# Five norms' sums of squares on four column groups of TensorE, with a copy and a fold

## The reference

```python
def rmsnorm(x, g):
    x32 = x.astype(jnp.float32)
    y = x32 * lax.rsqrt(jnp.mean(x32 * x32, axis=-1, keepdims=True) + EPS)
    return (y * g.astype(jnp.float32)).astype(x.dtype)

x = x + mix(rmsnorm(x, norm_mix_g[l])) @ w_out
x = x + conv_ffn(rmsnorm(x, norm_ffn_g[l]), ffn_w_up[l], ffn_conv_w[l], ffn_conv_b[l], ffn_w_down[l])
```

## Time and profile before

| | |
|---|---|
| median of three runs | 1513.62 us (1512.83 to 1514.57) |
| profiled execution, its own time | 1513.27 us |
| its span, first to last instruction | 1511.5 us |
| TensorE busy | 1461.0 us |
| VectorE busy | 1082.4 us |
| ScalarE busy | 732.3 us |
| mean granted TensorE clock | 0.989 of full |
| bytes moved | 274.79 MB, 182 GB/s |

### The profile page before, as it was taken

How to read it: one execution, slowest core, us unless ns; L and a number is a source line. 1 busy time by engine, 2 the same in 40 slices (tenths; PEclk the granted TensorE clock), 3 DMA queues, 4 the chain that set the end, 5 groups by cost and what they waited for, 6 DMA issues and landing times.

```text
span 1511.5 us, 26784 instructions
## 1 busy us (share of the span) xinstructions
PE 1461.0 (97%) x10486; PEld 1298.9 (86%) x10486; DVE 1082.4 (72%) x1659; ACT 732.3 (48%) x949; POOL 6.8 (0%) x19
## 2 busy tenths in 40 slices
PE   7989999999999999999999999899999999999997
PEld 7887889999987889999888779679999899799997
DVE  6774778778756787777766666667777768677775
ACT  6553545444545555445555433545444433454442
POOL 0000000000000000000000000000000000000000
PEclk9999999999999999999999999999999999999999
DMA  7433645555556344554526566055455554555551
GB/s 279 154 140 130 259 167 189 197 177 189 190 200 259 132 176 169 194 192 168 215 85 223 199 248 237 20 199 199 172 190 182 203 201 167 185 200 174 192 180 43
DMA packets 39677, 274.79 MB, mean 182 GB/s; under 512 B 4528, under 2 KB 5680, under 8 KB 6960
## 3 DMA queue, kind: packets, MB, share of 16 engines
q1 hardware_dynamic: 38304, 265.82, 48.9%
q0 software_dynamic: 720, 6.82, 1.2%
q10 hardware_dynamic: 576, 1.05, 0.2%
HBM read 272.62 MB, written 1.05 MB: 181 GB/s over the span
## 4 chain that ended last, share of the span: by engine, by line
PE 86%; DVE 7%; DMA 3%; ACT 3%; issue 2%; SPq 0%; DVEq 0%; ACTq 0%
PE L L1750 25%; PE D L1750 16%; PE L L1938 15%; PE L L1944 8%; PE N L1938 5%; DMA raw<-in_units 3%; PE N L1944 3%; PE M L1838 2%; DVE wlo L972 2%; PE N L1846 2%; PE D L1938 1%; PE D L2212 1%; PE N L2225 1%; DVE arena L1049 1%; PE D L1944 1%
## 5 line engine op out<-in xcount | busy, mean ns | idle before, releaser
L1750 PE MATMUL L<-h_all,whi 128*128 128x256 f32 (+1 forms) x1392 | 286.5, 305 | 14.9 <-DVE wlo L1258 7.0
L972 DVE TENSOR_TENSOR wlo<-raw,whi 128x2048 fp32r<-128x2048 f32 x106 | 242.3, 2286 | 76.9 <-ACT whi L492 76.5
L492 ACT ACTIVATE whi<-raw 128x2048 fp32r<-128x2048 f32 x106 | 202.0, 1909 | 120.7 <-PE L L1750 75.6
L1938 PE MATMUL L<-h_all,whi 128*128 128x512 f32 x992 | 252.7, 396 | 4.4 <-DVE h_all L1021 3.2
L1750 PEld LDWEIGHTS L<-h_all,whi 128*128 128x128 f32 x1392 | 228.3, 197 | 32.4 <-issue 16.4
L1134 DVE TENSOR_TENSOR wlo<-raw,whi 128x2048 fp32r<-128x2048 f32 x96 | 219.6, 2288 | 39.3 <-ACT whi L626 39.3
L1938 PEld LDWEIGHTS L<-h_all,whi 128*128 128x128 f32 x992 | 178.7, 190 | 41.4 <-DVE h_all L1021 5.1
L1750 PE MATMUL L<-h_all,wlo 128*128 128x256 f32 (+1 forms) x696 | 209.7, 301 | 0.0
L626 ACT ACTIVATE whi<-raw 128x2048 fp32r<-128x2048 f32 x96 | 182.9, 1905 | 0.0
L1750 PE MATMUL D<-hd_hi,whi 128*128 128x256 f32 x640 | 181.3, 283 | 0.0
L1750 PE MATMUL D<-hd_hi,wlo 128*128 128x256 f32 x640 | 181.1, 283 | 0.0
(11 more groups left out here) (305 smaller groups left out, 2269.0 us busy)
## 6 DMA issues: line engine op xcount, KB each, us to landing
raw<-in_units SPq DMA_DIRECT2D x250, 1024.0 KB, 4.9
arena<-in_band POOLq DMA_DIRECT2D x1, 2304.0 KB, 10.3
arena<-in_nax POOLq DMA_DIRECT2D x1, 1536.0 KB, 6.7
t<-in_mem ACTq DMA_DIRECT2D x4, 256.0 KB, 5.8
raw<-in_units SPq DMA_DIRECT2D x4, 256.0 KB, 5.4
x<-in_x SPq DMA_DIRECT2D x1, 1024.0 KB, 9.1
t<-in_ctx POOLq DMA_DIRECT2D x1, 1024.0 KB, 5.3
arena<-in_ctx POOLq DMA_DIRECT2D x1, 1024.0 KB, 7.4
```

Of the source, the lines that this page charges most:

```text
L492: A.activation(whi[weight_slot(v)][:], raw[v % RING][:], ACT.Copy).then_inc(unit_hi, 1)
L972: V.tensor_tensor(wlo[w][:], raw[v % RING][:], whi[w][:].bitcast(FP), ALU.subtract) \
L1750: ins = mm(dst, w[a], h[b], start=start and n == 0, stop=stop and n == 2, skip_group_check=True)
L1938: mm(bank[:], w[0][:, k, part * P:part * P + P], h_all[:, k, 0:512], start=k == 0, stop=False, skip_group_check=True)
```

## The change

TensorE's eight full products of a norm become eight products with 32 columns of ones, on four column groups: group g sums blocks 2g and 2g+1 into the output rows 32g to 32g+31 (`partial_sums`). VectorE copies the result to `var` (`gather`), and TensorE adds the four groups by one full product of ones with the copy (`fold_sums`). As each partial sum stands in 32 rows, the fold gives 32 times the sum, and the variance divides by 32 D. It applies to norms 1 to 5 above; the norms before ffn2, o_b and ffn3, the final one and the one after ffn1 keep `sums`. The places change too: for norms 3 and 5 all products now stand in the first chunk of the feed-forward layer and none between the jobs of a_out and b_out; the fold stands behind that chunk's `rest`. For norm 2 the fold stands behind the first job of a_out, its variance step behind the evacuation of that job, and ScalarE's root behind it too. For norm 4 the fold stands between kv_k0 and b_qm; for norm 1 right behind the partial sums.

```diff
@@ scalar
             jobs("mv1")
-            root(rs2)
             def a_rows(n, j):
+                if n == 0:
+                    root(rs2)
                 square(x, n)
@@ vector
+            def gather():
+                gathered[0] += 1
+                dve.wait_ge(R["ss_part"], gathered[0])
+                V.tensor_copy(var[:], N0[:, 0:T]).then_inc(R["ss_copy"], 1)
...
-            def residual(name, gate=None, g=None):
+            def residual(name, gate=None, g=None, behind_first=None):
...
+                if behind_first:
+                    hooks[0] = behind_first
@@ vector, ffn
                 upto(u0 + 2)
                 if not scaled:
-                    stat()
+                    gather()
+                    stat(32 * D)
                     dve.wait_ge(R["rs_done"], stats[0])
@@ vector, norms 2 and 3
-            stat()
+            gather()
             modulation(0, 0, 16, 1, [(0, 8, 1, "mix_w2", 0), (1, 8, 0, "mix_w2", 0)], fin=1)
-            residual("a_out", g=lambda k: vc("ffn_g", k))
+            residual("a_out", g=lambda k: vc("ffn_g", k), behind_first=lambda: stat(32 * D))
@@ tensor
-            def last_sums():
-                sums(2)
-                sums(3)
+            def partial_sums():
+                for i in range(2):
+                    for g in range(4):
+                        if i == 0:
+                            pe.wait_ge(R["sq_done"], 4 * stats[0] + g + 1)
+                        ins = mm(N0[32 * g:32 * g + 32, 0:T], ones[:, 0:32], sq[:, 2 * g + i, :],
+                                 start=i == 0, stop=i == 1)
+                ins.then_inc(R["ss_part"], 1)
+                parts[0] += 1
+            def fold_sums():
+                pe.wait_ge(R["ss_copy"], parts[0])
+                mm(N0[:, 0:T], ones[:, 0:P], var[:], start=True, stop=True).then_inc(R["ss_done"], 1)
+                stats[0] += 1
...
                     for part in range(2):
                         rest(w, ffn_bank(0, part), part)
+                    if mid:
+                        fold_sums()
...
             job(JOBS["mk0"][0], True, ready=first_ready)
-            stat()
+            partial_sums()
+            fold_sums()
             jobs("mv0")
...
-            stat()
-            residual("a_out", lambda k: MIX["memA"] + (k // 3 + 1 if k < 6 else 0), [6, 7, 0, 1, 2, 3, 4, 5], late=True)
-            ffn("ffn0", 0, last_sums, behind=None)
-            jobs("kv_k0", fresh=True, mid=stat)
+            partial_sums()
+            residual("a_out", lambda k: MIX["memA"] + (k // 3 + 1 if k < 6 else 0), [6, 7, 0, 1, 2, 3, 4, 5],
+                     after={0: fold_sums})
+            ffn("ffn0", 0, partial_sums, behind=None)
+            jobs("kv_k0", fresh=True, mid=partial_sums)
+            fold_sums()
             jobs("b_qm", fresh=True)
...
-            residual("b_out", b_mixed, [6, 7, 0, 1, 2, 3, 4, 5], late=True, begun=B_BEGUN)
-            ffn("ffn1", 1, last_sums, behind=boundary_sums)
+            residual("b_out", b_mixed, [6, 7, 0, 1, 2, 3, 4, 5], begun=B_BEGUN, after={})
+            ffn("ffn1", 1, partial_sums, behind=boundary_sums)
```

More of the change, by code:

```diff
@@ L384, in build @@
         R = {n: sem(n) for n in (
-            "ones_set", "sc_clear", "cc_ready", "rows_clear", "ada_out", "ada_turned", "ctx_hi", "ctx_lo", "piece_hi", "piece_lo", "sq_done", "ss_done", "rv_done", "rs_done", "t_done",
+            "ones_set", "sc_clear", "cc_ready", "rows_clear", "ada_out", "ada_turned", "ctx_hi", "ctx_lo", "piece_hi", "piece_lo", "sq_done", "ss_part", "ss_copy", "ss_done", "rv_done", "rs_done", "t_done",
             "h_hi_done", "h_lo_done", "rs_turn", "ctx_t", "sg_done", "v1_done", "rs1_done", "x_ready", "mod_ready", "q_silu", "o_sig",
@@ L958, in _ @@
             V = nc.vector
-            steps, made, stats, applied, rounded = [0], [0], [0], [0], [0]
+            steps, made, stats, applied, rounded, gathered = [0], [0], [0], [0], [0], [0]
             def step(ins):
@@ L1120, in evac @@
                     return V.scalar_tensor_tensor(d[1], b[:, T:512], gate(2 * n + 1), d[1], ALU.mult, ALU.add)
-                jobs(name, evac, {} if g is None else {n: (lambda n=n: rows(n - 1)) for n in range(1, 4)})
+                hooks = {} if g is None else {n: (lambda n=n: rows(n - 1)) for n in range(1, 4)}
+                if behind_first:
+                    hooks[0] = behind_first
+                jobs(name, evac, hooks)
                 if g is not None:
@@ L1744, in _ @@
             mm = nc.tensor.matmul
-            stats, h_in = [0], [0]
+            stats, parts, h_in = [0], [0], [0]
             def mm3(dst, w, h, start, stop):
@@ L1849, in sums, with residual @@
                     stats[0] += 1
-            def stat():
-                for i in range(4):
-                    sums(i)
-            def last_sums():
-                sums(2)
-                sums(3)
-            def residual(name, mixed, order=range(KB), late=False, begun={}):
+            def partial_sums():
[11 more added lines that the diff above has]
+                stats[0] += 1
+            def residual(name, mixed, order=range(KB), begun={}, after=None):
                 if name == "e_out":
                     pe.wait_ge(R["mix_lo_done"], MIX["na"])
[L1864 to L1867, removed]
+                if after is None:
+                    after = {1: lambda: sums(0), 2: lambda: sums(1)}
+                jobs(name, after=after, mixed=mixed, order=order, begun=begun)
+                if after and 1 in after:
+                    sums(2)
+                    sums(3)
             def attention(tl, t0, g0, mixbase, banks, beside={}, after={}, mixed=None, lead=False):
```

## The result

The changed kernel takes 1525.32 us (median of five runs, 1521.72 to 1526.45) against 1513.17 us before (five runs, 1511.86 to 1514.57): a ratio of 1.0076, 95% interval 1.0060 to 1.0092. That is 0.76% slower, some 12 us. The forecast was 1523.9, slower.

The account below looks back on a forecast made before the run. TensorE, busy 97% of the span, was taken as the bound. Terms of +1.15, -0.3, +2.2 and +2.1 gave +5.15 us, clock +5.1; together +10.25 on 1513.27 gave 1523.5, median 1523.9, range 1518.3 to 1527.0.

Parts of the forecast that it names:

- The prices: Sums of each norm: 3.69 us becomes 1.49 (partial sums 1.03, fold 0.46), 2.2 us of products less per norm.
- Norm 1: Norm of x at the start: copy queued behind a low part, variance step at 19.69 instead of 18.55, +1.15 us.
- C2: Rival: a slow stretch twice as long, or one at norm 1 that shows; +1.7 us or more, chance 0.07.
- Norms 2 and 3: Norms of ctx and ffn0: TensorE arrives 2.4 us early at the first down product and waits; gain only 0.3 us.
- The slack of 0.1 us: ffn0's entry: spare time between VectorE's read of Dn, semaphore included, and the first down product, 0.1 us.
- Norm 4: Norm of kv: fold waits for a copy behind a low part; b_qm +2.2 us later, after 4.1 us idle.
- Norm 5: ffn1's entry: variance step at 533.8 instead of 531.56, first down product +2.1 us later, TensorE idle 2.4 us.
- The clock: Four new TensorE gaps each followed by half clock; norm 1's hidden, the other three cost 1.7 us each, +5.1.
- rival A: One or two of three slow stretches don't come, 1520.5 to 1522.2 us, chance 0.25; none, 1518.8, chance 0.10.
- D: Rival: the copy ends before TensorE reaches the fold everywhere, only products count; 11 us faster, 1502.6 us, chance 0.04.
- B: Rival: lateness of norms 1 and 4 is taken up in the second attention; 2 to 5 us less, chance 0.08.
- C: Rival: loads of the 32 columns hide behind nothing; 0.3 us more per partial sum, 1524.5 us, chance 0.05.

Follow-up runs that it names:

- e1: Changed kernel with VectorE's copy of norm 4 moved ahead of the low part of kv_v0: 1521.05 us, 1.0041 of the kernel before.
- e3: Changed kernel with norms 3 and 5 undone (full sums, no copy, no fold): 1519.46 us, 1.0037 of the kernel before.
- e4: Changed kernel with nine idle full products of ones between kv_k0 and the fold of norm 4: 1521.33 us, 1.0056 of the kernel before.
- e10: Changed kernel with the fold of norms 3 and 5 between the two halves of the first chunk's low products: 1519.98 us, one run.
- e5: Changed kernel with norm 1 alone undone (eight full products, no copy, no fold): 1522.59 us, 1.0053 of the kernel before.
- e8: Changed kernel with the copy of norm 1 ahead of the low part of unit 1 in VectorE's queue: 1522.66 us, 1.0062 of the kernel before.
- e2: Changed kernel with partial sums made by full products of 128 columns, places, copies and folds kept: 1528.46 us, 1.0095 of the kernel before.
- e6: Kernel before with norm 2 changed and norm 4 changed with the copy ahead of the low part: 1515.74 us, 1.0012 of the kernel before.

## Why the prediction was right, point by point

**The prices.** Partial sums of 1.03 and a fold of 0.46: measured 1.00 and 0.45. The load of 32 columns takes 109 ns, between 90 and 190 as bounded. The rule of the Trainium skill ("TensorE: Matmul & The Clock Gate", Part 3, The mechanism), by which loads to the same row group don't overlap and the sums would take an estimated 1.4, doesn't hold here: the trace has 1.00. The same section also lets a load into a background weight buffer go ahead, which would fit; no run here tells whether that is what happens.

**Norm 1** was the term that was mis-sized: +1.15 forecast, +2.37 measured. The queue was read right (the copy at 18.81 behind the low part), but the fold was put at 0.61 us and took 1.22: TensorE's gap had already brought the clock to half when it began (0.78 in the two microseconds before it). In the profile of e1 norm 1 is that of the changed kernel, but the clock was still full in the two microseconds before the fold (1.00) and in it:

```profile
19.09 0.70 PE L1878 MATMUL N<-var,ones 128*128 128x256 f32 x2 [2.36 <-DVE var L1001]
```

From the start of the copy to the variance step it is 1.21 us there (18.62 to 19.83) and 1.73 in the changed kernel, and the first scores stand at 37.02, 1.28 after the kernel before. With the gap filled the term is 1.25. So about 1.2 is what copy and fold cost, as forecast, and 0.5 is the fold at half clock, which the forecast overlooked: it didn't see that the fold itself lies on the path. The rest: the low part ahead of the copy began 0.26 later in this profile (16.60, 16.34 before), and 0.38 more is lost between VectorE's evacuation (33.87) and the scores, 4.24 us where e1 and the kernel before have 3.86. The forecast called the slow stretch of norm 1 hidden and reckoned with 3.4 us of it; this one fills the whole of 19 to 25 (0.50) and shows. e3, e4 and e10, also with a fold of 1.2 us at half clock, have 4.34, 4.06 and 4.15 there. So the last case of C2 (a slow stretch at norm 1 that shows) came in part, with 0.9 us and not 1.7.

**Norms 2 and 3**: -0.3 forecast, +0.17 measured. The parts are as worked out: sums -1.17 (forecast -1.3), from a_out's start to ffn0's chunk -1.07 (25.54 to 24.47), chunk to down +2.30, and 0.12 ahead of the sums. The step from chunk to variance was 7.49, forecast 7.45. The saved microseconds reached the down product and waited there for 2.28 us, 2.4 forecast. The slack of 0.1 us that the prediction read from the chain wasn't there (see e10); the rest of what the term is off by is the 0.1 or so that each part fell short.

**Norm 4**: +3.9 forecast with the clock, +3.89 measured; gap 4.41, forecast 4.1. b_qm starts 2.22 us later behind kv_k0 (13.22 and 11.00), 2.2 forecast, and filling the gap gives back 1.48 of clock, 1.7 forecast. The agreement to 0.01 is luck all the same: against the same stretch at full clock (16.40) the loss is 4.34, and in e5 and e10, whose clock behind and within the gap was lower for longer (0.57 over eight microseconds, 402 to 410 and 403 to 411), the same code takes 21.51 and 22.03.

**Norm 5**: +2.1 forecast, +2.30 measured, gap 2.27.

**The clock**: three stretches beyond norm 1's were forecast, two came in this profile. Of the twelve gaps of 2.3 us ahead of a first down product (six profiles with two each) seven were followed by half clock; of the five unfilled gaps of 4.1 to 4.4 us at norm 4 all five. Shorter gaps are as uneven: the one of 1.78 us ahead of kv_k0 is followed by half clock in the kernel before and not in the changed one. So for gaps of 2.3 us rival A was about as likely as the forecast, and the chance that all three come was set too high.

**The sum** came out near for a reason that wasn't forecast. The three clock terms were put at 5.1 us and brought some 3.0 (1.48 at norm 4, 1.48 in ffn1's loop, nothing in ffn0's). The terms without them were put at 5.15 and brought 7.25 (2.37, 0.17, 2.41 and 2.30): norm 1 alone cost 1.2 more. These two errors cancel, and that is luck. What is left, +1.97 in stretches that the diff doesn't touch (+0.08, +0.83 and +1.06 in the table, with half clock in other places), stands in no term. So the median is 1.4 us above 1523.9. The mechanism, waits behind the copy and behind the rigid stretch, is what e1, e3, e5, e8 and e10 show; its size to a microsecond isn't earned.

**The rivals.** D (only products count) is out by e2 and e3: at norm 4 longer products only take the place of waiting (20.74 us both times), and full sums make the entries faster. B (lateness taken up in the second attention) is out: the turn to b_out is 76.73 us after 76.68. But its mirror image is real: an earlier arrival there is given back, 0.71 of 1.17 us in e1 and all of it in e6. C (loads that hide behind nothing) is out by the 1.00 us of the sums. Of A, one slow stretch of the three didn't come.

## What to carry to other kernels

A step that becomes three with an engine change between them (product, copy, fold) is only as good as the place of the copy in the other engine's queue: at norm 4 the same instructions cost 3.9 us behind a 2.3 us low part and gained 1.2 ahead of it (and lost that again further on). Before work is taken off the busiest engine, look for the next thing that it waits for and ask who sets that; here a rigid way of VectorE and ScalarE, which already set the time, made the 2.3 us by which TensorE came earlier to ffn0's down product worth nothing. And a gap of 2.3 us in TensorE can cost 1.5 more in clock (ffn1's loop, 172.21 and 170.72), or nothing (ffn0's).

## What the runs showed that was not expected

Unchanged stretches move with the clock from one kernel to the next: from the first scores to the first ada product the twelve profiles give 90.09 to 94.39 us for the same instructions, and the two of before and after happen to agree (92.81 and 92.89). The five runs of the changed kernel fall into 1521.7 to 1521.9 with a mean clock of 0.988 and 1525.3 to 1526.5 with 0.983 to 0.985. For effects under 3 us the distances between landmarks tell more than the medians.

Idle work can pay: 4.1 us of products into a bank that nobody reads, in norm 4's gap, made TensorE 1.5 us earlier. And the way back from column groups to full products costs about 0.2 us (1.14 against 0.92 for the same four records, and 0.92 again in e2 behind full products).
